# Expert rows of a MoE layer: scattered by owner from the pool engine instead of stored slot by slot from the scalar engine

## The reference

```python
gi = jnp.argmax(lg, axis=-1)                       # one of 4 groups
top_v, top_i = lax.top_k(le_g, TOP_K)              # two of its 8 experts
wts = (pg_top[:, None] * jax.nn.softmax(top_v, axis=-1)).reshape(-1)
eid = (gi[:, None] * EXP_PER_GROUP + top_i).reshape(-1)
...
hid = jax.nn.silu(xb @ w_g[e]) * (xb @ w_u[e])
return hid @ w_d[e]
...
return jnp.zeros((n, d), xt.dtype).at[t_s].add(yd[dest] * w_s[:, None])
```

## Time and profile before

| | us |
|---|---|
| three timed runs | 1437.19, 1437.69, 1440.59 |
| median | 1437.69 |
| the profiled execution, its own time | 1435.27 |
| its span, first to last instruction | 1433.4 |

### The profile page before, as it was taken

The page is one execution under the profiler, slowest core; times in us unless marked ns, Lnnn a source line. Parts: engine busy times, 40 slices in busy tenths (PEclk is TensorE's granted clock), DMA queues, the critical chain, the costliest instruction groups (busy, mean ns, idle before and its releaser), DMA issues. The chain is left out here.

```text
span 1433.4 us, 22234 instructions
## 1 busy us (share of the span) xinstructions
PE 1208.5 (84%) x8870; PEld 911.5 (64%) x8870; DVE 632.4 (44%) x1445; ACT 455.6 (32%) x1043; POOL 138.1 (10%) x175
## 2 busy tenths in 40 slices
PE   5999898999998739999988379988998587888871
PEld 3788754888878636556565278856998564445540
DVE  1545686454444582222221375575777732221213
ACT  3533466433343420001000274255665300000002
POOL 2410010111103130000000201001011000000001
PEclk9999999999999869999999779999999799999996
DMA  9952389523323128999999584268554179999994
GB/s 350 320 164 84 100 295 318 147 88 102 105 88 148 59 38 339 403 414 396 410 419 408 208 246 131 87 249 266 177 180 146 72 299 424 421 422 423 422 421 143
DMA packets 128928, 356.03 MB, mean 248 GB/s; under 512 B 20457, under 2 KB 82145, under 8 KB 104257
## 3 DMA queue, kind: packets, MB, share of 16 engines
q1 hardware_dynamic: 116560, 317.68, 59.6%
q0 software_dynamic: 6528, 18.59, 4.2%
q10 hardware_dynamic: 5744, 18.43, 3.3%
HBM read 332.62 MB, written 22.06 MB: 247 GB/s over the span
## 5 line engine op out<-in xcount | busy, mean ns | idle before, releaser
L1778 DVE TENSOR_TENSOR w_lo<-ring,w_hi 128x256 fp32r<-128x256 f32 x480 | 222.7, 474 | 239.7 <-ACT w_hi L1412 238.6
L1412 ACT ACTIVATE w_hi<-ring 128x256 fp32r<-128x256 f32 x480 | 197.4, 417 | 301.6 <-PE banks L917 253.2
L1146 PE MATMUL banks<-ring,arena 128*64 128x256 f32 x2048 | 231.8, 381 | 38.1 <-issue 16.1
L917 PE MATMUL banks<-h_hi,w_hi 128*128 128x512 f32 (+1 forms) x640 | 221.9, 347 | 7.0 <-DVE h_lo L1709 5.7
L1146 PEld LDWEIGHTS banks<-ring,arena 128*64 128x64 f32 x2048 | 153.4, 137 | 107.4 <-issue 27.9
L917 PE MATMUL banks<-h_lo,w_hi 128*128 128x512 f32 (+1 forms) x640 | 220.5, 345 | 0.0
L917 PE MATMUL banks<-h_hi,w_lo 128*128 128x512 f32 (+1 forms) x640 | 220.2, 344 | 0.0
L1160 PE MATMUL banks<-ring,att 128*64 128x512 f32 x512 | 123.7, 627 | 29.8 <-issue 19.3
L917 PEld LDWEIGHTS banks<-h_hi,w_hi 128*128 128x128 f32 x640 | 122.8, 192 | 23.4 <-ACT arena L1383 5.4
L1544 ACT ACTIVATE arena<-banks 128x1024 f32<-128x1024 f32 x32 | 32.8, 1026 | 313.4 <-PE banks L1160 313.4
L917 PEld LDWEIGHTS banks<-h_hi,w_lo 128*128 128x128 f32 x640 | 122.9, 192 | 14.0
(11 more groups left out here) (219 smaller groups left out, 1503.5 us busy)
## 6 DMA issues: line engine op xcount, KB each, us to landing
ring<-in_w_e_gate SPq DMA_DIRECT2D x64, 1024.0 KB, 8.9
ring<-in_w_e_up SPq DMA_DIRECT2D x64, 1024.0 KB, 9.7
ring<-in_w_e_down SPq DMA_DIRECT2D x64, 1024.0 KB, 10.2
ring<-in_w_mod SPq DMA_DIRECT2D x48, 1024.0 KB, 6.3
ring<-in_w_in SPq DMA_DIRECT2D x38, 1024.0 KB, 6.9
expert_rows<-arena ACTq DMA_DIRECT2D x32, 512.0 KB, 8.2
ring<-in_w_o SPq DMA_DIRECT2D x8, 1024.0 KB, 5.1
ring<-in_w_branch SPq DMA_DIRECT2D x8, 640.0 KB, 4.9
```

The costliest lines, as they stand in the source:

```text
L917: ins = mm(out_ap, a, b, start=k == 0 and p_ == 0, stop=k == KD - 1 and p_ == 2)
L1146: ins = mm(banks[e * CAP:(e + 1) * CAP, bank, 0:DE], x[:, k, e * CAP:(e + 1) * CAP], w[:, k * DE:(k + 1) * DE], start=k == 0, stop=k == KD ...
L1412: fn(w_hi[:, u % AHEAD, :, :], chunk(key)[:, q * KU:(q + 1) * KU, :], ACT.Copy).then_inc(w_hi_ready, 1)
L1778: v.tensor_tensor(w_lo[:, u % AHEAD, :, :], chunk(key)[:, q * KU:(q + 1) * KU, :], w_hi[:, u % AHEAD, :, :].bitcast(F32), ALU.subtract).th ...
```

## The change

ACT only copies the rows (`take_y`). The rows are written by POOL with an indirect DMA (`put_rows`), whose list of row numbers is, for each slot, the number of the pair that holds it, 2 x token + choice. A slot that no pair holds has the number NOWHERE, which is out of bounds and is not written. The list is made in HBM (`slot_owner`): filled with NOWHERE at the start (`blank_owners`, 2 DMAs), then written by pair with indirect DMAs of 4-byte elements (8 in layer 0, 4 in layer 1) and loaded back as 128 x 16 integers (`set_owners`). `yd` now has 1024 pair rows and 1024 spill rows, and `zero_rows` zeroes all of them. The gathers go by `back_u`: the pair's own row, or for a spilled pair its spill row; DVE works this out in five more small steps in `place`, between `select(l, 0)` and `meta`. The small loads and the strips of layer 1, which POOL issued right after `slots_ready`, are now issued between the puts: the small loads after the second put, two strip DMAs after each of the next six.

```diff
-ROWS_D = MAIN + SPILL[0] * CAP
+ROWS_D = 2 * NTOK + SPILL[0] * CAP
+NOWHERE = 1 << 20
...
-        ZEROED = 16 * (ROWS_D - MAIN) // P
+        ZEROED = 16 * ROWS_D // P
...
-                for r in range(MAIN // P, ROWS_D // P):
+                for r in range(ROWS_D // P):
                     pool.dma_start(yd[r * P:(r + 1) * P, :], zero).then_inc(yd_zero, 16)
+            def blank_owners():
+                pool.memset(pair_own[:, :], NOWHERE).then_inc(nowhere_ready, 1)
+                pool.wait_ge(nowhere_ready, 1)
+                for l in range(DEPTH):
+                    pool.dma_start(owner[l].rearrange("(p r) s -> p (r s)", p=P), pair_own[:, :]).then_inc(owner_blank, 16)
+            def set_owners(l):
+                pool.wait_ge(own_ready, 1)
+                pool.wait_ge(owner_blank, 16 * DEPTH)
+                pool.wait_ge(slots_ready, l + 1)
+                for c in range(2):
+                    for tt in range(QT[l]):
+                        pool.indirect_dma_start(
+                            out=owner[l], out_offset=bass.IndirectOffsetOnAxis(ap=slots_u[:, c, tt:tt + 1], axis=0),
+                            in_=own_u[:, c, tt:tt + 1], in_offset=None, bounds_check=MAIN - 1, oob_is_err=False)\
+                            .then_inc(owner_set[l], 16)
+                pool.wait_ge(owner_set[l], 32 * QT[l])
...
+                pool.dma_start(pair_own[:, :], owner[l].rearrange("(n p) s -> p (n s)", p=P), allow_slow_non_contiguous=True).then_inc(pair_own_in[l], 16)
+                pool.wait_ge(pair_own_in[l], 16)
+            def put_rows(l, p):
+                n = E0[l] + p
+                pool.wait_ge(y_out, n + 1)
+                pool.indirect_dma_start(
+                    out=yd, out_offset=bass.IndirectOffsetOnAxis(ap=pair_own[:, p:p + 1], axis=0),
+                    in_=y_sb[n % 2], in_offset=None, bounds_check=2 * NTOK - 1, oob_is_err=False)\
+                    .then_inc(y_stored[n % 2], 16)
...
+                pool.wait_ge(back_ready, l + 1)
                 pool.wait_ge(rows_done, l + 1)
...
-                            in_offset=bass.IndirectOffsetOnAxis(ap=slots_u[:, c, tt:tt + 1], axis=0))\
+                            in_offset=bass.IndirectOffsetOnAxis(ap=back_u[:, c, tt:tt + 1], axis=0))\
...
-                if l == 0:
-                    pool.wait_ge(slots_ready, 1)
-                    small_loads(pool, 1)
-                    load_rev(pool, 1)
+                set_owners(l)
+                for p in range(NPAIR):
+                    put_rows(l, p)
+                    if l == 0 and p == 1:
+                        small_loads(pool, 1)
+                    if l == 0 and 2 <= p < 2 + H_NA:
+                        load_rev(pool, 1, (p - 2,))
                 combine(l)
...
-                act.wait_ge(y_out, lin(i, n + 1, PPI))
-                act.dma_start(yd[bass.ds(row, P), :], y_sb[b]).then_inc(y_stored[b], 16)
...
                 select(l, 0)
+                own = C["own"].rearrange("p (c t) -> p c t", c=2)[:, :, 0:nt]
+                back = back_f[:, :, 0:nt]
+                link(v.tensor_scalar(back, slots_f[:, :, 0:nt], float(2 * NTOK - MAIN), None, ALU.add))
+                link(v.tensor_tensor(back, back, own, ALU.subtract))
+                link(v.tensor_tensor(back, back, ge, ALU.mult))
+                link(v.tensor_tensor(back, back, own, ALU.add))
+                if l:
+                    dve.wait_ge(got_in[QT[0] - 1], 32)
+                v.tensor_copy(back_u[:, :, 0:nt], back).then_inc(back_ready, 1)
```

More of the change, by code:

```diff
@@ L104, in constants @@
     c["thr"] = np.tile(np.arange(1, NBK) * CAP, (P, 1))
+    c["own"] = 2 * (np.arange(4)[None, None] * P + p[:, None, None]) + np.arange(2)[None, :, None]
+    c["own"] = c["own"].reshape(P, 8)
     return np.concatenate([c[n].astype(np.float32) for n in CONST_COLS], axis=1)
@@ L284, in program @@
         yd = nc.dram_tensor("expert_rows", (ROWS_D, D), F32, kind="Internal").ap()
+        owner = [nc.dram_tensor(f"slot_owner{l}", (MAIN, 1), U32, kind="Internal").ap() for l in range(DEPTH)]
         mod_rows = nc.dram_tensor("mod_rows", (DEPTH, 6, 2, D), F32, kind="Internal").ap()
@@ L327, in program @@
         slots_u = sb("slots_u", [P, 2, 4], U32)
+        own_u = sb("own_u", [P, 2, 4], U32)
+        back_f = sb("back_f", [P, 2, 4])
+        back_u = sb("back_u", [P, 2, 4], U32)
+        pair_own = sb("pair_own", [P, NPAIR], U32)
         wts = sb("wts", [P, 2, 4])
@@ L477, in program @@
         yd_zero = sem("yd_zero")
+        nowhere_ready = sem("nowhere_ready")
+        own_ready = sem("own_ready")
+        owner_blank = sem("owner_blank")
+        owner_set = [sem(f"owner_set{l}") for l in range(DEPTH)]
+        pair_own_in = [sem(f"pair_own_in{l}") for l in range(DEPTH)]
+        back_ready = sem("back_ready")
         th_hi_ready = sem("th_hi_ready")
@@ L817, in _ @@
             ffn_scale_rows()
+            blank_owners()
             zero_rows()
@@ L1534, in silu, with take_y @@
                 fn(act_g[n % 2], banks[:, G_BANK, 0:DE], ACT.Silu).then_inc(silu_ready, 1)
-            def store_y(l, p, i=None):
+            def take_y(l, p, i=None):
                 n = E0[l] + p
-                row = p * P if i is None else act.snap(i * (PPI * P) + p * P)
                 b = n % 2
@@ L1551, in experts @@
                     silu(l, p + 1)
-                    store_y(l, p)
+                    take_y(l, p)
                 with act.Fori(0, LOOPED) as i:
@@ L1555, in experts @@
                         silu(l, p + 1, i)
-                        store_y(l, p, i)
+                        take_y(l, p, i)
                 for p in range(TAIL, NPAIR):
@@ L2202, in _ @@
                 gates(l)
+                if l == 0:
+                    v.tensor_copy(own_u[:, :, :], C["own"].rearrange("p (c t) -> p c t", c=2)).then_inc(own_ready, 1)
                 residual(l)
```

7 lines of the change are left out of this document (5 added, 2 removed).

## The result

| us | before | after |
|---|---|---|
| median of the timed runs | 1437.78 (1437.19 to 1440.59, 4 runs) | 1458.46 (1456.23 to 1460.20, 4 runs) |
| the profiled execution, its own time | 1435.27 | 1459.86 |
| its span | 1433.4 | 1457.7 |

A forecast was written before the change was run, and what follows sets the result against it. The DMA engines were taken to set the pace in both layers' experts. -5.5 - 9.4 + 7.0 + 2.0 + 0.2 + 3.4 = -2.3 us took 1435.27 to 1433.0; 2.4 more for the median gave 1435.4, range 1422 to 1446.

The forecast's parts named there:

- The moved loads: Layer 1's small and strip loads, issued in layer 0's full experts' stretch: +7.0 us, ends 3.4 and 10.1.
- The saving in layer 1: Experts of layer 1: unowned rows skipped leave the fullest DMA engine 68 of 128 rows, -9.4 us.
- the dealing in runs of four: Experts' stores: rows go to DMA engines in runs of four neighbours; 5.5 us saved in layer 0, 9.4 in layer 1.
- the first test: Whole kernel: HBM written near 15.8 MB; near 22 + 4 MB would mean nothing is skipped.
- The rival in which the saving isn't there: Experts' stores: unowned slots cost the fullest engine as before, leaving only costs, +12.6 us, 1450.3; 20 in 100.
- The saving in layer 0: Experts of layer 0: unowned rows skipped leave the fullest DMA engine 94 of 128 rows, -5.5 us.
- Even dealing (rival): Experts' stores: rows shared evenly over the engines, -10.4 and -15.1 us by layer, total -12.9, 1424.8; 25 in 100.
- The head: Before the experts: five more DVE steps, 1.0 us per layer, and layer 0's `own_u` copy, 0.2 us at most.
- The tails: After each layer's last down product: POOL's indirect write lands later than a direct store, 1.7 us per layer, +3.4.
- What I cost at nothing: Extra zero rows, owner lists, POOL's added issues and waits, and the puts themselves: all taken as hidden, 0 us.
- The zeros: At 55 to 80 us: 4.2 MB more zero rows, hidden behind PE's computing, 0 us; 10 us without that cover.
- The owner list: Before layer 0's experts: list ready at about 545 us, first put wanted at 562, 50 us of cover; 0 us.

The follow-up runs named there:

- the even layout: Changed kernel with layer 1's loads issued early again, and slots renumbered so an expert's neighbouring slots lie four partitions apart: 1432.25 us, ratio 0.9976.
- the last version: Changed kernel with loads early, slots renumbered over partitions, five steps behind the copies, and pair rows numbered choice x 512 + token: 1429.86 us, ratio 0.9925.

## Why the prediction was wrong, step by step

**The moved loads, +7.0 (ends 3.4 and 10.1): measured +21 to +27.** This is the step that failed, and nearly alone: 18.2 of the 26.6 us between forecast and trace are in that one stretch, whose pairs took 19.6 us, 3.4 more than those behind them, where some 1 us more was expected. Both of its rows were read rightly as far as they went. The earlier trace rows has the same loads of layer 0 beside weights, at a share of 1.10 and 242 GB/s, and the price taken from there, 7, is near the 8.7 of the one experiment that is like that row: a burst. What I did not see is that the row does not stand for the form of the change. It prices one burst of twelve in order of heads, and in that form the strips took at most 5.2 us of engine time; the change issues six couples, the two halves of a head each time, and so they took 19.4. The upper end came from the loads running alone, which is no bound either for loads that return beside a full stream: 10.1 us of all engines alone, 19.4 for the strips by themselves here. An end of a range that is taken from a quieter stretch bounds nothing from above.

**The saving in layer 1, -9.4: measured -9.1.** By its own steps: 15.6 us a pair as written, and the even layout moved it as the dealing in runs of four says. The 16.8 - 6.3 MB less and the 4.2 MB more zeros show in the DMA packets, 356.03 MB before and 349.78 after. They don't show in "HBM written", on which I had put the first test: it rose by 4.2 MB. In the trace's DMA records a put leaves a packet of 4096 bytes for each owned row and one of 4 bytes, some 9 ns long, for each unowned one; "HBM written" counts the put's full shape. The rival in which the saving isn't there is out, though its 1450.3 lay nearer the result than my forecast. Over all traces the stretch of the measured 9.1, first to sixteenth copy, is 231.2 to 233.2 us with all rows written and 221.8 to 224.3 with rows skipped.

**The saving in layer 0, -5.5.** The changed kernel without the moved loads has L0 6 us below before, but not for my reason: with all rows written it is shorter still. So the size agrees by luck. The margin of 1.3 us a pair to PE's pace, some 20 us for sixteen, would not have capped a term of 5.5. What the sum lacked is that the stores from POOL, and a rest of 6 us that stays open, bring layer 0 to PE's pace by themselves, so that skipped rows have nothing left to save there.

**Even dealing (rival).** Not what the chip does. As an edit, it brought 3.1 of the 4.3 us worked out for twelve pairs of layer 1.

**The head, +2.2: measured about +5.7.** In layer 0 PE comes to the same pick at 533.1 instead of 531.4, of which 0.6 us are there before the slots are known. In layer 1 the steps themselves are near the size that I gave: the pause between the first group of picks and the second grows from 1.22 to 2.46 us. After the pause, though, PE's matmuls run slower. The second group in the kernel before, then after (start, us, wait in brackets):

```profile
1147.96 0.38 PE L1138 MATMUL banks<-att_r,h_hi 128*128 128x256 f32 x1 [1.22 <-DVE arena L2091]
1148.18 0.28 PE L1138 MATMUL banks<-att_r,h_lo 128*128 128x256 f32 x1
1148.30 0.28 PE L1138 MATMUL banks<-att_r,h_hi 128*128 128x256 f32 x1
```

```profile
1176.76 0.39 PE L1191 MATMUL banks<-att_r,h_hi 128*128 128x256 f32 x1 [2.46 <-DVE arena L2151]
...
1177.70 0.42 PE L1191 MATMUL banks<-att_r,h_hi 128*128 128x256 f32 x1
1177.92 0.41 PE L1191 MATMUL banks<-att_r,h_lo 128*128 128x256 f32 x1
```

The table by stretch from the pick on, before and after, gives the granted clock, the third number from the end:

```profile
1147.90:1152.90 5.00, 3.75 (x32) 3.28 (x34) 2.84 (x7) 0.00 (x0) 0.00 (x0) 1.00 0.00 0
```

```profile
1176.70:1181.70 5.00, 3.77 (x19) 3.34 (x21) 2.89 (x7) 0.00 (x0) 1.24 (x1) 0.57 0.11 2
1181.70:1186.70 5.00, 5.00 (x38) 3.35 (x36) 0.00 (x0) 0.26 (x1) 0.00 (x0) 0.75 0.00 0
```

In the first five microseconds the clock was 1.00 before and 0.57 after, mostly at the lower level of 1.2 GHz, and PE got through 19 matmuls instead of 32. With the five steps behind the copies it was 1.00 again. From this pick to the first product with weights it is 3.3 to 3.4 us in all six traces without the steps in front of the copies, and 3.8 to 4.7 in the fourteen with them. To the first copied rows it is 25.4 us in all four traces that have no such steps at all, 26.5 to 28.0 in thirteen of the fourteen (32.0 in the one with the even layout). The clock of the five microseconds from the pick is 1.00 in the six and 0.56 to 0.66 in the fourteen. So five small steps cost 1.2 us themselves and in those thirteen 1.1 to 2.6 more behind the pause, beside a lower clock. To move them didn't win that back, as the 29.3 and, in the last version, 27.5 us show.

**The tails, +3.4 for both layers: measured +3.6 and +1.9 by stretch.** The chain of waits at the end of the changed kernel, beside the earlier trace rows:

```profile
1426.96 1.03 ACT arena L1595
...
1428.78 3.35 DMA expert_rows<-arena,pair_own
...
1434.13 1.00 POOL att L858
1435.14 0.25 issue
...
1435.44 5.87 DMA att<-expert_rows,back_u
```

From the start of the copy to the first gather it is 7.17 us (5.80 before), in layer 0 7.91 (5.66); from the copy's end, as the prediction counts, 6.1 in layer 1, where it had 6.4. The landing itself is 3.35 instead of 2.82; the rest is that POOL begins the put 0.8 us after the copy's end. A direct store from POOL already has 6.8 to 6.9 us there, so some 1.1 us go with POOL in each layer, and 0.3 and 1.1 with the indirect form, in single traces. To this come 0.5 to 1.0 us from the first gather to the first weighing, which I had at nothing. The tail of layer 0 is 24.7 us in the second trace of the unchanged kernel as against 20.7 in the first, so its +3.6 is no sharper than that; likewise 2.5 of the 3.9 us before layer 1's pick lie in attention and mixers, which both kernels share, and are in that second trace too (330.2 us for the stretch).

**What I cost at nothing.** The zeros: the drift between the two kernels' matmuls is 0.3 us at 112 us, behind them. The owner list: its load was issued at 536.7 us, long before the first put at 564.8. POOL's queue: never late, as its timeline shows. With the loads early the owner list's load, 2048 pieces of 4 bytes, is issued at 551 to 560 us, beside the first weights, and from the slots to the first copy of layer 0 it takes 41.9 to 44.5 us in the five traces of such versions, where the changed kernel has 40.1: putting the loads back has a price of 2 to 4 us here, within the net gain above. That the list's load is what costs them wasn't tested.

## What to carry to other kernels

When loads are moved from an idle stretch into one where the DMA engines are full, price their **form**, not their bytes: the engine time of their queue in a stretch (share times length) per MB, read where they run beside such a stream, in the same order and the same portions. Small pieces that overlap and are shifted against one another were 3 to 4.5 times as dear as the same pieces laid apart when they came two to a put, and hardly dearer in one burst; put such loads where the engines are idle, or all at once. And a saving of bytes counts only on the fullest engine and only down to the next engine's pace, so lay out the rows that are left before counting them.

## What the runs showed of the hardware

- 1.18 MB in 4608 pieces of 256 bytes, read beside a full stream: 4.3 us of sixteen engines when they lay apart or all on one address, 13.2 to 19.4 us when they overlapped at shifts of 4 bytes, two loads after each of six puts. In one burst the latter took at most 5.2. In the stretch with the 19.4 us all engines together moved 340 GB/s at a share of 0.97, without the strips 403 at 1.00.
- A row that an indirect write skips for its number leaves a packet of some 9 ns, where a row of 4 KB takes some 160.
- Renumbering the slots alone took 3.1 us off twelve pairs of layer 1 (187.3 to 184.2).
- ACT was held 35.9 us by issuing twelve loads of 384 pieces each beside a full stream, 20.4 us by one of them; POOL issued the same twelve in 7.95.
- After a pause of 2.46 us, where the kernel before had 1.22, between two groups of picks, PE's next five microseconds had a granted clock of 0.57, where they had 1.00.
